# RWKV state chain: two of the three products of each step summed in PSUM ahead of the chain, and one direction's u moved to other banks

## The reference, cut to what matters

```python
def step(S, inp):
    r_t, lw_t, k_t, v_t, kk_t, a_t = inp
    s_kk = jnp.einsum('bhvk,bhk->bhv', S, kk_t)
    S = (S * jnp.exp(lw_t)[:, :, None, :]
         - s_kk[..., None] * (a_t * kk_t)[:, :, None, :]
         + v_t[..., None] * k_t[:, :, None, :])
    return S, jnp.einsum('bhvk,bhk->bhv', S, r_t)
...
o_cf, s_cf = scan_fn(*cf, s0)      # context, forward
o_lf, _ = scan_fn(*lf, s_cf)       # latents, from the context's last state
o_cb, s_cb = scan_fn(*cb, s0)      # the same, backward
o_lb, _ = scan_fn(*lb, s_cb)
```

## Time and profile before

| | us |
|---|---|
| median of 3 runs | 2376.91 |
| lowest and highest of them | 2373.87, 2386.03 |
| the profiled execution, own time | 2386.95 |
| its span, first to last instruction | 2385.1 |

### The profile page before, as it was taken

How to read it: one execution, slowest core, us unless ns; L and a number is a source line. 1 busy time by engine, 2 the same in 40 slices (tenths; PEclk the granted TensorE clock), 3 DMA queues, 4 the chain that set the end, 5 groups by cost and what they waited for, 6 DMA issues and landing times. The chain is left out here.

```text
span 2385.1 us, 50237 instructions
## 1 busy us (share of the span) xinstructions
PE 2180.2 (91%) x21268; PEld 1843.5 (77%) x21268; DVE 1350.5 (57%) x1956; ACT 971.2 (41%) x1385; POOL 370.6 (16%) x347
## 2 busy tenths in 40 slices
PE   7888999899999999999999998788888988998998
PEld 3555777778788688878888877577777877898998
DVE  5436575665466534464444456566666555567666
ACT  4534333232454232342322437434343454345544
POOL 0002221412234200000000000132233155100000
PEclk9998999999999999999999999899999989898999
DMA  7531412314211123322222232200000122355553
GB/s 284 193 124 58 152 66 106 134 55 152 72 62 58 67 97 101 136 81 97 98 97 97 97 144 94 85 12 28 20 12 29 38 71 67 112 185 182 175 182 125
DMA packets 64734, 241.32 MB, mean 101 GB/s; under 512 B 7296, under 2 KB 8448, under 8 KB 63104
## 3 DMA queue, kind: packets, MB, share of 16 engines
q1 hardware_dynamic: 62064, 218.66, 26.8%
q10 hardware_dynamic: 2448, 19.46, 2.1%
HBM read 231.80 MB, written 6.29 MB: 100 GB/s over the span
## 5 line engine op out<-in xcount | busy, mean ns | idle before, releaser
L397 PE MATMUL psum<-normed_high,weights_high 128*128 128x512 f32 (+1 forms) x1552 | 569.4, 367 | 19.7 <-DVE weight_ring_parts L1031 17.0
L1031 DVE TENSOR_TENSOR weight_ring_parts<-weight_ring,weights_high 128x1024 fp32r<-128x1024 f32 (+1 forms) x327 | 417.0, 1275 | 263.8 <-ACT weights_high L1544 256.5
L398 PE MATMUL psum<-normed_low_part,weights_high 128*128 128x512 f32 (+1 forms) x1552 | 555.9, 358 | 0.0
L399 PE MATMUL psum<-normed_high,weight_ring_parts 128*128 128x512 f32 (+1 forms) x1552 | 554.2, 357 | 0.0
L1544 ACT ACTIVATE weights_high<-weight_ring 128x1024 fp32r<-128x1024 f32 (+1 forms) x327 | 340.0, 1040 | 188.2 <-PE psum L399 136.7
L397 PEld LDWEIGHTS psum<-normed_high,weights_high 128*128 128x128 f32 x1552 | 306.7, 198 | 76.7 <-DVE weight_ring_parts L1031 27.7
L398 PEld LDWEIGHTS psum<-normed_low_part,weights_high 128*128 128x128 f32 x1552 | 306.2, 197 | 39.9 <-issue 2.0
L399 PEld LDWEIGHTS psum<-normed_high,weight_ring_parts 128*128 128x128 f32 x1552 | 305.1, 197 | 40.7
L470 PE MATMUL psum<-work 64*64 64x64 f32 (+1 forms) x7040 | 245.4, 225 | 33.0 <-issue 10.9
L470 PEld LDWEIGHTS psum<-work 64*64 64x64 f32 x7040 | 234.6, 136 | 51.8 <-issue 38.6
L397 PE MATMUL psum<-hidden_high,weights_high 128*128 128x512 f32 (+1 forms) x512 | 172.4, 337 | 3.7 <-DVE hidden_low L1486 3.7
(11 more groups left out here) (249 smaller groups left out, 3479.1 us busy)
## 6 DMA issues: line engine op xcount, KB each, us to landing
weight_ring<-in_weights SPq DMA_DIRECT2D x407, 512.0 KB, 3.5
x_scratch<-work ACTq DMA_DIRECT2D x2, 2048.0 KB, 11.7
weight_ring<-in_weights SPq DMA_DIRECT2D x16, 256.0 KB, 2.6
work<-x_scratch ACTq DMA_DIRECT2D x2, 2048.0 KB, 9.2
work<-in_ret_constants ACTq DMA_DIRECT2D x2, 1152.0 KB, 16.1
work<-in_x ACTq DMA_DIRECT2D x1, 2048.0 KB, 10.9
work<-in_small_weights ACTq DMA_DIRECT2D x1, 1152.0 KB, 6.6
constants<-in_constants ACTq DMA_DIRECT2D x1, 1024.0 KB, 8.9
```

What stands on the lines that cost most here:

```text
L397: mm(ps, w[0][:, cols], x[0], start=first, stop=False)
L398: mm(ps, w[0][:, cols], x[1], start=False, stop=False)
L399: return mm(ps, w[1][:, cols], x[0], start=False, stop=last)
L1031: tt(ring_r[:, i % RING, o], ring[:, i % RING, o], high[:, n % HIGHS, o].bitcast(F32), ALU.subtract).then_inc(vec_split.sem, vec_split.ste ...
```

## The change

1. `uk` of direction 1 goes to a second pair of banks, `low_pair` (0 and 1), and no longer shares banks 2 and 3 with direction 0.
2. The state sums of a direction get one bank for the whole chain (banks 4 and 5, one for each direction), with 64 columns for each chunk. Before the chain, the keys-by-values products of steps 0 to 6 of both directions are put there, and then the b-by-u products are added. Only the first of a direction clears the bank; the rest are written with no start mark.
3. `pt` and `rr` move from `mid` to the four banks `big` (0 to 3). The order on TensorE becomes `pt` of direction 0, keys-by-values of both directions, `pt` of direction 1, b-by-u of both directions, `rr` of both. The helper functions are `inverse_product` and `added`.
4. A chain step is now: for each direction wait for S(i), then the one product with S(i) for each head; after both directions, the output products of both, with the wait for the last S and for the corrected queries moved behind the first two of them.
5. VectorE drains `pt` of both directions ahead of the chain, and `rr` behind the two S of step 0.

The number of products is the same. The core of the diff:

```diff
-        wide = banks(2, 1, 2)
+        wide, low_pair = banks(2, 1, 2), banks(0, 1, 2)
...
+                    def added(ps, d, m, t, lhs, rhs, start):
+
+                        for h in range(2):
+                            q = slice(64 * h, 64 * h + 64)
+                            last = mm(ps[q, 64 * t:64 * t + 64], lhs(q, m), rhs(q, m), start=start, stop=False, skip_group_check=True)
+                        return last
+
+                    def inverse_product(d):
+
+                        B = RW_D[d]
+                        eng.wait_ge(act_rwkv.sem, act_rwkv.at("drained", "uk", l, c, d))
+                        ps = big.fill("pt", l, c, d)
+                        for free in big.freed():
+                            eng.wait_ge(*free)
+                        per_head(ps, 64, cell(B + LT, 128, 64), cell(B + BTT)).then_inc(mid_filled.sem, mid_filled.step(("pt", l, c, d)))
+
+                    big.start_at(2)
+                    mid.start_at(0)
+                    inverse_product(0)
+                    for d in range(2):
+                        ps = mid.fill("dS", l, c, d)
+                        for free in mid.freed():
+                            eng.wait_ge(*free)
+                        for i in range(M - 1):
+                            m = chain_order(d)[i]
+                            added(ps, d, m, m, cell(RW_D[d] + KTT), cell(RW_VT), i == 0)
+                    inverse_product(1)
+                    for d in range(2):
+                        for i in range(M - 1):
+                            m = chain_order(d)[i]
+                            last = added(mid.get("dS", l, c, d), d, m, m, cell(RW_D[d] + BTT), cell(RW_D[d] + LT, 128), False)
+                        last.then_inc(mid_filled.sem, mid_filled.step(("dS", l, c, d, 0)))
...
-                            if i < M - 1:
-                                if i > 0:
-                                    eng.wait_ge(vec_rwkv.sem, vec_rwkv.at("S", l, c, d, i))
-                                if i == 1:
-                                    eng.wait_ge(vec_rwkv.sem, vec_rwkv.at("drained", "pt", l, c, d))
-                                ps = mid.fill("dS", l, c, d, i)
-                                for free in mid.freed():
-                                    eng.wait_ge(*free)
...
+                            if i == 1:
+                                eng.wait_ge(vec_rwkv.sem, vec_rwkv.at("drained", "pt", l, c, d))
+                            if 0 < i < M - 1:
+                                eng.wait_ge(vec_rwkv.sem, vec_rwkv.at("S", l, c, d, i))
+                                last = added(mid.get("dS", l, c, d), d, m, m, cell(B + MT), lambda q, m: work[q, B + YK + 64 * i:B + YK + 64 * i + 64], False)
                                 last.then_inc(mid_filled.sem, mid_filled.step(("dS", l, c, d, i)))
...
+                            added(ps, d, m, m, cell(RW_VT), cell(B + AKT), i == m0)
+                            last = added(ps, d, m, m, cell(B + LT, 128), cell(B + ABT), False)
+                            if i == M - 1:
+                                eng.wait_ge(vec_rwkv.sem, vec_rwkv.at("S", l, c, d, i))
+                            if i == max(m0, 1):
                                 eng.wait_ge(vec_rwkv.sem, vec_rwkv.at("drained", "rr", l, c, d))
```

More of the change, by code:

```diff
@@ L698, in _ @@
                         eng.wait_ge(vec_rwkv.sem, vec_rwkv.at("drained", "dR", l, c, d, 5))
-                        ps = wide.fill("uk", l, c, d)
-                        for free in wide.freed():
+                        ps = (wide, low_pair)[d].fill("uk", l, c, d)
+                        for free in (wide, low_pair)[d].freed():
                             eng.wait_ge(*free)
                         per_head(ps, 128, cell(B + RR), cell(B + YK, 128, 0, 128)).then_inc(wide_filled.sem, wide_filled.step(("uk", l, c, d)))
+                    def added(ps, d, m, t, lhs, rhs, start):
[3 more added lines that the diff above has]
+                        return last
@@ L703, in _ @@
                     for d in range(2):
                         B = RW_D[d]
-                        eng.wait_ge(act_rwkv.sem, act_rwkv.at("drained", "uk", l, c, d))
-                        ps = mid.fill("rr", l, c, d)
-                        for free in mid.freed():
+                        ps = big.fill("rr", l, c, d)
+                        for free in big.freed():
                             eng.wait_ge(*free)
                         per_head(ps, 64, cell(B + LT, 128, 64), cell(B + ABT), m0).then_inc(mid_filled.sem, mid_filled.step(("rr", l, c, d)))
-                        ps = mid.fill("pt", l, c, d)
@@ L711, in _ @@
-                        for free in mid.freed():
-                            eng.wait_ge(*free)
-                        per_head(ps, 64, cell(B + LT, 128, 64), cell(B + BTT)).then_inc(mid_filled.sem, mid_filled.step(("pt", l, c, d)))
                     for d in range(2):
@@ L721, in _ @@
                             m = chain_order(d)[i]
-                            if i < M - 1:
-                                if i > 0:
-                                    eng.wait_ge(vec_rwkv.sem, vec_rwkv.at("S", l, c, d, i))
-                                if i == 1:
-                                    eng.wait_ge(vec_rwkv.sem, vec_rwkv.at("drained", "pt", l, c, d))
-                                ps = mid.fill("dS", l, c, d, i)
[L728 to L739, removed]
+                            if i == 1:
[3 more added lines that the diff above has]
+                                last = added(mid.get("dS", l, c, d), d, m, m, cell(B + MT), lambda q, m: work[q, B + YK + 64 * i:B + YK + 64 * i + 64], False)
                                 last.then_inc(mid_filled.sem, mid_filled.step(("dS", l, c, d, i)))
-                            if i == M - 1:
-                                eng.wait_ge(vec_rwkv.sem, vec_rwkv.at("S", l, c, d, i))
+                        for d in range(2):
+                            B = RW_D[d]
+                            m = chain_order(d)[i]
                             if m < m0:
@@ L745, in _ @@
                             ps = outb.get("O", l, c, d)
-                            if i == m0:
-                                eng.wait_ge(vec_rwkv.sem, vec_rwkv.at("drained", "rr", l, c, d))
[L748 to L758, removed]
+                            added(ps, d, m, m, cell(RW_VT), cell(B + AKT), i == m0)
[3 more added lines that the diff above has]
+                            if i == max(m0, 1):
+                                eng.wait_ge(vec_rwkv.sem, vec_rwkv.at("drained", "rr", l, c, d))
+                            if i > 0:
+                                last = added(ps, d, m, m, lambda q, m: work[q, B + YK + 64 * i:B + YK + 64 * i + 64], cell(B + KR, 128, 64), False)
                             if i == M - 1:
@@ L1341, in _ @@
                         B = RW_D[d]
[L1342 to L1345, removed]
                         eng.wait_ge(mid_filled.sem, mid_filled.at("pt", l, c, d))
-                        tt(chunks(B + MT), ident64(kc), mid.get("pt", l, c, d).rearrange("p (m t) -> p m t", t=64),
+                        tt(chunks(B + MT), ident64(kc), big.get("pt", l, c, d).rearrange("p (m t) -> p m t", t=64),
                                     ALU.add).then_inc(vec_rwkv.sem, vec_rwkv.step(("drained", "pt", l, c, d)))
@@ L1355, in _ @@
                             eng.wait_ge(mid_filled.sem, mid_filled.at("dS", l, c, d, i))
-                            ts(wk(B + YK + 64 * (i + 1), 64), mid.get("dS", l, c, d, i)[:, 0:64],
+                            ts(wk(B + YK + 64 * (i + 1), 64), mid.get("dS", l, c, d)[:, 64 * m:64 * m + 64],
                                         work[:, B + WW + e:B + WW + e + 1], None, ALU.mult).then_inc(vec_rwkv.sem, vec_rwkv.step(("S", l, c, d, i + 1)))
                             eng.wait_ge(vec_rwkv.sem, vec_rwkv.n)
-                            vec_rwkv.also(("drained", "dS", l, c, d, i))
+                            if i == M - 2:
+                                vec_rwkv.also(("drained", "dS", l, c, d))
+                        if i == 0:
+                            for d in range(2):
+                                B = RW_D[d]
+                                eng.wait_ge(mid_filled.sem, mid_filled.at("rr", l, c, d))
+                                tt(chunks(B + KR, 64, 64, 128, m0), chunks(B + KR, 64, 64, 128, m0),
+                                            big.get("rr", l, c, d).rearrange("p (m t) -> p m t", t=64)[:, m0:, :], ALU.add).then_inc(vec_rwkv.sem, vec_rwkv.step(("drained", "rr", l, c, d)))
+                                eng.wait_ge(vec_rwkv.sem, vec_rwkv.n)
                     eng.wait_ge(out_filled.sem, out_filled.at("O", l, c, 0))
@@ L1803, in _ @@
                         eng.wait_ge(wide_filled.sem, wide_filled.at("uk", l, c, d))
```

(2 more changed lines are left out.)

## The result

The changed kernel takes 2356.91 us (median of 4 runs, 2355.46 to 2359.95) against 2377.3 us before (4 runs); the ratio is 0.9906 with a 95% interval of 0.9888 to 0.9924. That is 20 us gained, where 15 were forecast. The profiled execution took 2357.53 us with a span of 2355.7.

What follows compares the result with a forecast made beforehand. TensorE, the busiest engine, was taken as the bound, by its pace or waits. Savings of 13.2 us by waits and 16.2 laid out gave 15: 2376.91 - 15 = 2362 us, range 2354 to 2375.

Steps and rivals of the forecast that it cites:

- What bounds the pass: In the eight passes: TensorE's own pace in layer 0's chain, 0.029 us a record; in layer 1 without outputs, the TensorE-VectorE-TensorE round trip.
- the turnaround: In the chain, from TensorE's first record through VectorE's scaling back to TensorE: a direction's cycle falls from 1.24 to 0.88 us.
- the waits ahead of the chain: TensorE waiting for drains between `uk` and the chain; none left after the change, 2.0 us saved in layer 0, 2.7 in layer 1.
- The bank pair: Before the chain, `uk` of direction 1 waits 1.44 us a pass for the banks shared with direction 0.
- The chain with outputs: Steps 1 to 6 in layer 0, 4 to 6 in layer 1: 32 records, taking 0.94 and 1.07 us in turns.
- The step that S(2) loses to the `rr` drain: Layer 1's step 2: `rr`'s second drain stands ahead of S(2) on VectorE, which comes at 8.4 and not 8.1 us.
- Layer 0's sum: Layer 0's pass laid out record by record: 15.7 us against 17.64.
- Halving the difference of two sums: Savings of 13.2 us by waits and 16.2 laid out, differing by about 0.4 us of seams between record groups; 15 taken.
- The rival on the clock: Layer 1's thinned steps halve TensorE's clock for 6.8 us, costing 4.5 us a pass, 18 in all: 2380 us; chance 0.07.
- The total: Whole kernel: 15 us gained, 2362 us against the median; chance 0.62 of faster by over 0.5%.
- more is gained: Rival: lagging direction costs nothing, steps reach matmul pace; another 0.6 us in layer 0, 1.2 in layer 1: 2355 us; chance 0.15.
- The way from one pass to the next: From L1362 of one pass to L1804 of the next: growing longer would say the gain was given back in between.

## Why the prediction was right

**What bounds the pass: right.** TensorE's own pace was the bound in layer 0 and the turnaround in layer 1's first steps; the waits ahead of the chain were found but for one: in layer 0 `rr` of direction 1 waits 0.2 us for `mid`, inside the stretch of 160 records that was read as having no gap (records start 0.23 us apart at 395.5, where 0.03 is the pace). A record lasts 0.22 us, so the merged row hides it. After the change the start times of `pt`, keys by values, `pt`, b by u, `rr` and the chain, from the first drain on, are those laid out, to 0.1 us (keys by values at 2.4 for 2.5, the chain at 8.5 for 8.6).

**The bank pair: right in mechanism and size.** 1.44 us a pass was forecast, 1.48 is the difference with it undone and 1.35 to 1.48 with it alone.

**The chain with outputs: right.** Steps of 0.94 and 1.07 us in turns were forecast; the pairs of scalings stand 0.93, 0.99 and 0.94 apart in layer 0.

**The turnaround: one half mis-sized.** From the first of 4 records to the scaling it is 0.45 us, as taken. From the scaling to TensorE it is 0.34 and not the 0.43 of the earlier trace rows, so a cycle is 0.79 and not 0.88. The step that S(2) loses to the `rr` drain is there. Layer 1 was laid out at 14.4 us a pass and its passes at full clock take 13.94: 0.27 of that are three such cycles, the rest an S(2) that comes at 8.3 and not 8.4 us and an output step of 0.94 and not 1.07.

**Layer 0's sum: too small a gain by a term that was not in it.** 15.7 us was laid out and 15.49 came, but the kernel before was priced by its clean pass of 17.64 us. In three profiles with the old chain, 8 of 12 passes of layer 0 were 0.2 to 1.3 us longer than the clean one (a ninth by 0.06), 0.8 to 2.6 us an execution; with the new chain none of 32 is. Halving the difference of two sums, to leave seams in place, was the wrong way too: the seams went.

**The rival on the clock: its mechanism happened, at a third of its price.** It had a chance of 0.07. The granted clock fell to half in the output steps behind the thin ones, in up to three of four passes of layer 1, though the idle gaps there are under 0.7 us. It lasted 3.4 us and not 6.8, and cost 1.5 us a pass (15.43 - 13.94) and not 4.5. All 3.4 us lie on work that TensorE's pace bounds, and there 32 records take 1.71 us for 0.94, so 3.4 x (1 - 0.94 / 1.71) = 1.5. The 4.5 could not have come out of 6.8 us either: at 2 to 1 that is a loss of 3.4 at most. By the page of the Trainium skill that the prediction named (TensorE: Matmul & The Clock Gate, A second HAM failure mode), frequent short idle times between groups of matmuls can bring the clock to half too. The traces are in line with it, with idle times of 0.14 to 0.68 us in the steps ahead of the falls, where I had set the absence of a long gap against it.

**The total: near, in part by luck.** Within the passes the mean of two profiles before is 138.6 us and of three after 121.0: 17.6 us, against 15. Two errors partly cancel in it: passes without standstills and at full clock gain 18.9 us, the standstills add 1.7 on the mean, and the falls of the clock take 3.0. The gains in time were 20.4 us (interval 18.1 to 26.6) and 18.1 us (16.6 to 26.1); the 17.6 is within the second interval and just below the first. Forecast were 2362 us, a chance of 0.62 for faster by over 0.5%; it is faster by 0.94%. The 2357 and 2358 us that came are nearer to the 2355 of the rival "more is gained" than to the forecast, as the passes say too. The way from one pass to the next, whose lengthening was named as a sign of being wrong, did not grow.

**Open.** What holds TensorE up in the old chain, with its state ready, was not found; a shortage of instructions or the doubled order of waits are guesses that no run here separates. What decides in which pass the clock falls is open as well, and so is whether a few us between the passes belong to the change.

## What to carry to other kernels

In a serial chain, take out of each step every product that does not need the step's input, but leave enough independent work behind the dependent product: a step thinned to a few short matmuls gains nothing below the turnaround (0.79 us here, with 8 records or with 20), and it may cost TensorE its clock in what follows. Look for a second user of the same PSUM banks before looking at the chain; here other banks for one of two products gave half of the gain. Compare the same stretches of several profiles, for behind the last pass alone two profiles of one kernel differ by 6.6 us, for either kernel. And before a pass is called longer, look whether only the mark at its end has moved.

## What the runs showed of the hardware

The clock could fall behind three steps of 8 records of 64x64 products each, with idle gaps of no more than 0.7 us between them; with 12 more records a step it held in all four passes of one profile. At half clock 32 records took 1.71 us for 0.94, so a fall of 3.4 us cost 1.5. TensorE took up a product 0.34 us after the start of a 0.28 us VectorE instruction in the changed kernel (1601.05 - 1600.71), and 0.43 us after it in the kernel before; why is not shown. A chain of short products whose steps begin with a wait ahead of six of them had standstills, 0.2 to 1.3 us a pass, in 8 of 12 passes, the one looked at with the state ready; with the wait ahead of two of them there were none in 32 passes.
